# The final norm of a decoder layer, moved into the last expert group of its mixture-of-experts stage

## The reference

```python
def moe_ffn(h, w_router, b_router, w_gu, b_gu, w_down, b_down):
    ...
    xs = hf[tok]
    gu = lax.ragged_dot(xs, w_gu, group_sizes) + b_gu[sorted_e]
    gate, up = jnp.split(gu, 2, axis=-1)
    ...
    act = (up + 1.0) * (gate * jax.nn.sigmoid(SWIGLU_ALPHA * gate))
    out = lax.ragged_dot(act.astype(h.dtype), w_down, group_sizes) + b_down[sorted_e]
    out = out * weights.reshape(-1)[order][:, None]
    y = jnp.zeros((T, D), dtype=out.dtype).at[tok].add(out)

def reference(...):
    ...
    x = x + g2 * moe_ffn(h, ...)
    return rmsnorm(x, norm_f)
```

## Time and profile before

| | |
|---|---|
| median of three runs | 4119.27 us (4119.03 to 4123.2) |
| profiled execution | 4121.83 us, its span 4120.1 us |
| PE busy | 95% of the span |
| DVE, ACT, POOL busy | 57%, 37%, 14% |
| mean granted clock of TensorE | 0.976 |
| moved by DMA | 763.09 MB, mean 185 GB/s |

### The profile page before, as it was taken

How to read it: one execution, slowest core, us unless ns; L and a number is a source line. 1 busy time by engine, 2 the same in 40 slices (tenths; PEclk the granted TensorE clock), 3 DMA queues, 4 the chain that set the end, 5 groups by cost and what they waited for, 6 DMA issues and landing times. The chain is left out here.

```text
span 4120.1 us, 64304 instructions
## 1 busy us (share of the span) xinstructions
PE 3904.0 (95%) x18356; PEld 3205.4 (78%) x18357; DVE 2352.0 (57%) x3725; ACT 1530.1 (37%) x2258; POOL 567.1 (14%) x600
## 2 busy tenths in 40 slices
PE   7999999898979999999999999999999999999993
PEld 4888788787868878878778888878888788888782
DVE  5263342795765764554675666586565656444742
ACT  3222321662223542342453444364343434322532
POOL 1110110111221111101110201111110211111102
PEclk9999999899989999999999999999999999999997
DMA  6442441764345774565684777597575856544826
GB/s 240 156 133 87 156 142 57 251 208 153 133 143 186 244 266 122 153 221 137 201 280 165 222 241 229 151 344 226 167 222 177 258 166 220 163 122 114 268 96 188
DMA packets 347524, 763.09 MB, mean 185 GB/s; under 512 B 29849, under 2 KB 29906, under 8 KB 342818
## 3 DMA queue, kind: packets, MB, share of 16 engines
q1 hardware_dynamic: 289138, 600.04, 42.3%
q0 software_dynamic: 55120, 151.68, 15.0%
q10 hardware_dynamic: 3200, 10.53, 0.6%
HBM read 653.81 MB, written 108.33 MB: 185 GB/s over the span
## 5 line engine op out<-in xcount | busy, mean ns | idle before, releaser
L1860 ACT CAST weights_split<-weights_raw 128x1024 fp32r<-128x1024 f32 x420 | 431.4, 1054 | 536.3 <-PE tok_bank_acc L118 487.2
L116 PE MATMUL tok_bank_acc<-weights_first,weights_split 128*128 128x512 f32 x1264 | 506.2, 401 | 11.4 <-DVE weights_first L1953 9.3
L1953 DVE TENSOR_TENSOR weights_split<-weights_raw,weights_split 128x1024 fp32r<-128x1024 f32 x420 | 490.7, 1220 | 22.0 <-ACT weights_split L1860 13.0
L116 PE MATMUL tok_bank_acc<-weights_split 128*128 128x512 f32 x1264 | 498.4, 394 | 0.8 <-DVE weights_split L1953 0.8
L1953 DVE TENSOR_TENSOR weights_first<-weights_raw,weights_first 128x1024 fp32r<-128x1024 f32 x416 | 483.8, 1219 | 20.7 <-ACT weights_first L1860 18.8
L117 PE MATMUL tok_bank_acc<-weights_split 128*128 128x512 f32 x1264 | 495.6, 392 | 0.0
L118 PE MATMUL tok_bank_acc<-weights_split 128*128 128x512 f32 x1264 | 495.4, 392 | 0.0
L118 PE MATMUL tok_bank_acc<-weights_first,weights_split 128*128 128x512 f32 x1264 | 494.3, 391 | 0.0
L117 PE MATMUL tok_bank_acc<-weights_first,weights_split 128*128 128x512 f32 x1264 | 493.7, 391 | 0.0
L1838 POOL DMA_INDIRECT y_rows<-tok_act_row,tok_token x123 | 199.6, 1622 | 2130.3 <-DVE tok_act_row L2022 2080.7
L1860 ACT CAST weights_first<-weights_raw 128x1024 fp32r<-128x1024 f32 x416 | 425.5, 1050 | 168.8 <-PE tok_bank_acc L118 125.9
(11 more groups left out here) (327 smaller groups left out, 6594.1 us busy)
## 6 DMA issues: line engine op xcount, KB each, us to landing
weights_raw<-in_w_gu SPq DMA_DIRECT2D x560, 512.0 KB
weights_raw<-in_w_down SPq DMA_DIRECT2D x280, 512.0 KB
tok_bias<-in_b_gu SPq DMA_DIRECT2D x35, 1024.0 KB
early_w_raw<-in_w_in POOLq DMA_DIRECT2D x14, 2048.0 KB, 11.1
proj<-pro_stage SPq DMA_DIRECT2D x112, 256.0 KB, 2.0
pro_w_ada<-in_w_ada POOLq DMA_DIRECT2D x64, 256.0 KB, 3.5
mix_late<-proj SPq DMA_DIRECT2D x48, 256.0 KB, 3.7
mod_w_ada<-in_w_ada SPq DMA_DIRECT2D x8, 1024.0 KB, 16.0
```

The costliest lines, as they stand in the source:

```text
L116: nc.tensor.matmul(out, act_hi, w_hi, start=first, stop=False)
L1860: nc.scalar.copy(whi[c % 2][:, j * SK:(j + 1) * SK], raw[:, n % RAW]).then_inc(hi_done, 1)
L1953: nc.vector.tensor_tensor(wlo[c % 2][:, rows], raw[:, n % RAW], whi[c % 2][:, rows], ALU.subtract).then_inc(lo_done, 1)
```

## The change

The finish phase is gone as a phase. What it does is written into the turn of the last group (`G.nT < 1`) of the tokens phase, on the same engines but for the stores, which SP issues.

- **SP**, behind the last piece loads: waits until the group's tokens and shares are taken out of `rec`, loads norm_f into that buffer, waits until all scatters of earlier groups have landed, and loads y tile by tile into the eight weight slots, tile i when piece 16 + i is split. The 16 tiles go in four batches of four (`BATCH`): the stores of batch 0 and 1 must have landed before tiles 8 to 11 and 12 to 15 are loaded into their slots.
- **ACT** squares and takes roots by batch (`tiles_rms`): batch 0 behind the last weight copy, batches 1 to 3 behind the last activation copy. The squares are written to the PSUM bank `tx`; sums and roots lie in parts of `bias`.
- **DVE** inverts and multiplies in place (`tiles_out`): batch 0 in front of `weigh(NGU, 0)`, batches 1 to 3 behind the additions of the first half and in front of `weigh(NGU + 1, 0)`.
- **The tokens of the last group** are not scattered with addition. POOL gathers their sums so far from y into `xs` (eight gathers). DVE adds each weighed half (`add_prior`), ACT squares the whole rows, DVE normalizes them, and POOL writes them to `out` by index, when all stores of tiles have landed, so that they replace what the tiles left there. POOL waits for these writes inside the group's turn.
- The waits for `y_out` at POOL's end are gone, and `weigh(NGU + 1, t)` of the other groups stands inside their `nT > 0` block.

```diff
+                with sp.If(G.nT < 1):
+                    sp.wait_ge(token_set, g + 1)
+                    sp.sem_inc(wait_carrier, 1)
+                    sp.wait_ge(share_set, g + 1)
+                    sp.dma_start(norm_f, A["norm_f"].partition_broadcast(P)).then_inc(nf_in, 16)
+                    for half in range(2):
+                        sp.wait_ge(y_out[half], G.landed(0))
+                        sp.sem_inc(wait_carrier, 1)
+                    def load_tile(i):
+                        for half in range(2):
+                            sp.dma_start(raw[:, i % RAW, half], y_t[half][:, i]).then_inc(fin_in[i // BATCH], 16)
+                    def store_tiles(b):
+                        for i in range(b * BATCH, (b + 1) * BATCH):
+                            sp.wait_ge(z_done, i + 1)
+                            sp.dma_start(out_t[:, i], whole(i)).then_inc(fin_out[b], 16)
+                    for i in range(RAW):
+                        sp.wait_ge(lo_done, G.pieces(PIECES * NCH - RAW + i + 1))
+                        load_tile(i)
+                    for b in range(2):
+                        store_tiles(b)
+                        sp.wait_ge(fin_out[b], 16 * BATCH)
+                        for i in range(RAW + b * BATCH, RAW + (b + 1) * BATCH):
+                            load_tile(i)
+                    for b in range(2, NT // BATCH):
+                        store_tiles(b)
...
+                with pool.If(G.nT < 1):
+                    pool.wait_ge(tx_done, G.before + G.T + 1)
+                    for t in range(GT):
+                        with pool.If(G.T > t):
+                            for half in range(2):
+                                pool.indirect_dma_start(
+                                    out=xs[:, t, half * N:(half + 1) * N], out_offset=None, in_=keep["y"][half],
+                                    in_offset=bass.IndirectOffsetOnAxis(ap=token[:, t:t + 1], axis=0)
+                                    ).then_inc(prior_in, 16)
+                    for done in fin_out:
+                        pool.wait_ge(done, 16 * BATCH)
+                    for t in range(GT):
+                        with pool.If(G.T > t):
+                            pool.wait_ge(last_row, t + 1)
+                            pool.indirect_dma_start(
+                                out=out_rows, out_offset=bass.IndirectOffsetOnAxis(ap=token[:, t:t + 1], axis=0),
+                                in_=xs[:, t], in_offset=None, bounds_check=S - 1, oob_is_err=False).then_inc(row_out, 16)
+                    pool.wait_ge(row_out, G.T * 16)
-        for half in range(2):
-            pool.wait_ge(y_out[half], total * 16 + 16)
...
+                def square_sum(rows, i):
+                    nc.scalar.activation(junk, rows, ACT.Square, accum_out=ssq[:, i:i + 1]).then_inc(sq_done, 1)
+                    act.wait_ge(sq_done, i + 1)
+                def tiles_rms(b):
+                    act.wait_ge(fin_in[b], 32 * BATCH)
+                    for i in range(b * BATCH, (b + 1) * BATCH):
+                        square_sum(whole(i), i)
+                    cols = slice(b * BATCH, (b + 1) * BATCH)
+                    nc.scalar.activation(rms[:, cols], ssq[:, cols], ACT.Sqrt, scale=1.0 / D,
+                                         bias=const("eps")).then_inc(rms_done, 1)
...
                 for n in range(5 * PIECES + PIECES // 2, 6 * PIECES):
                     weights_hi(g, n, G.chunks_before(NGU))
+                with act.If(nT < 1):
+                    tiles_rms(0)
                 for t in range(1, GT):
                     with act.If(G.T > t):
                         activations_hi(1, t)
...
+                with act.If(nT < 1):
+                    for b in range(1, NT // BATCH):
+                        tiles_rms(b)
+                    for t in range(GT):
+                        with act.If(G.T > t):
+                            act.wait_ge(sum_done, G.T + (t + 1))
+                            square_sum(xs[:, t], NT + t)
+                            nc.scalar.activation(rms[:, NT + t:NT + t + 1], ssq[:, NT + t:NT + t + 1], ACT.Sqrt,
+                                                 scale=1.0 / D, bias=const("eps")).then_inc(last_rms, 1)
...
                 for n in range(5 * PIECES + PIECES // 2, 6 * PIECES):
                     weights_lo(g, n)
+                with dve.If(nT < 1):
+                    tiles_out(0)
                 weigh(NGU, 0)
...
+                with dve.If(nT < 1):
+                    dve.wait_ge(prior_in, G.T * 32)
+                    for t in range(GT):
+                        with dve.If(G.T > t):
+                            add_prior(NGU, t)
+                    for b in range(1, NT // BATCH):
+                        tiles_out(b)
+                    for t in range(GT):
+                        with dve.If(G.T > t):
+                            weigh(NGU + 1, t, last=True)
+                            add_prior(NGU + 1, t)
+                    for t in range(GT):
+                        with dve.If(G.T > t):
+                            i = NT + t
+                            dve.wait_ge(last_rms, t + 1)
+                            nc.vector.reciprocal(rms[:, i:i + 1], rms[:, i:i + 1]).then_inc(last_inv, 1)
+                            dve.wait_ge(last_inv, t + 1)
+                            nc.vector.scalar_tensor_tensor(out=xs[:, t], in0=xs[:, t], scalar=rms[:, i:i + 1], in1=norm_f,
+                                                           op0=ALU.mult, op1=ALU.mult).then_inc(last_row, 1)
...
-def phase_finish(nc, k, A, keep):
...
-        run(phase_finish)
```

More of the change, by code:

```diff
@@ L1696, in expert_programs, with whole @@
     rows_left, LEFT = keep["rows_left"], 5
+    (nf_in, sq_done, rms_done, inv_done, z_done, prior_in, sum_done, last_rms, last_inv, last_row,
+     row_out) = k.sems("nf_in sq_done rms_done inv_done z_done prior_in sum_done last_rms last_inv last_row row_out")
+    BATCH = 4
+    fin_in = [k.sem(f"fin_in{b}") for b in range(NT // BATCH)]
+    fin_out = [k.sem(f"fin_out{b}") for b in range(NT // BATCH)]
+    y_t = [a.rearrange("(t p) n -> p t n", p=P) for a in keep["y"]]
+    out_t = keep["out"].rearrange("o (t p) d -> p (o t) d", p=P)
+    out_rows = keep["out"].rearrange("o s d -> (o s) d")
+    norm_f = rec[:].bitcast(F32).rearrange("p q c -> p (q c)")
+    junk = tx[:].rearrange("p a b c -> p (a b c)")
+    def whole(n):
+        return raw[:, n % RAW].rearrange("p s n -> p (s n)")
     y_out = [y_out0, y_out1]
@@ L1816, in gpsimd @@
         pool.wait_ge(rest_in, 16)
-        count, total = field(pool, 0, COUNT, NG), field(pool, 0, TOTAL, NG * GT)
+        count = field(pool, 0, COUNT, NG)
         with pool.Fori(0, NG) as g:
@@ L1832, in gpsimd @@
                 pool.sem_inc(wait_carrier, 1)
-                for c in (NGU, NGU + 1):
+                with pool.If(G.nT > 0):
+                    for c in (NGU, NGU + 1):
+                        for t in range(GT):
+                            with pool.If(G.T > t):
+                                pool.wait_ge(read_done, G.chunk_tile(c, t))
+                                pool.sem_inc(wait_carrier, 1)
+                                pool.indirect_dma_start(
+                                    out=keep["y"][c - NGU],
+                                    out_offset=bass.IndirectOffsetOnAxis(ap=token[:, t:t + 1], axis=0),
+                                    in_=weighted_at(c, t), in_offset=None, compute_op=ALU.add
+                                    ).then_inc(y_out[c - NGU], 16)
@@ L2010, in activations_lo, with tiles_out, add_prior, weigh @@
                     nc.vector.tensor_tensor(alo[:, t, s], ta[:], ahi[:, t, s], ALU.subtract).then_inc(alo_done, 1)
-                def weigh(c, t):
+                def tiles_out(b):
+                    cols = slice(b * BATCH, (b + 1) * BATCH)
+                    dve.wait_ge(rms_done, b + 1)
+                    nc.vector.reciprocal(rms[:, cols], rms[:, cols]).then_inc(inv_done, 1)
+                    dve.wait_ge(inv_done, b + 1)
+                    if b == 0:
+                        dve.wait_ge(nf_in, 16)
+                    for i in range(b * BATCH, (b + 1) * BATCH):
+                        nc.vector.scalar_tensor_tensor(out=whole(i), in0=whole(i), scalar=rms[:, i:i + 1], in1=norm_f,
+                                                       op0=ALU.mult, op1=ALU.mult).then_inc(z_done, 1)
+                def add_prior(c, t):
+                    cols = slice((c - NGU) * N, (c - NGU + 1) * N)
+                    dve.wait_ge(read_done, G.chunk_tile(c, t))
+                    nc.vector.tensor_tensor(xs[:, t, cols], xs[:, t, cols], weighted_at(c, t), ALU.add).then_inc(sum_done, 1)
+                def weigh(c, t, last=False):
                     dve.wait_ge(mm_done, G.chunk_tile(c, t))
@@ L2018, in weigh @@
                         dve.wait_ge(y_out[1], G.landed(0))
-                    if c == NGU + 1 and t == 1:
```

(16 more changed lines are left out.)

54 lines of the change are left out of this document (2 added, 52 removed).

## The result

The changed kernel takes 4462.0 us in the median (4457.3 to 4464.8), the kernel before 4119.6 in the same session: a ratio of 1.0829, with a 95% interval of 1.0816 to 1.0842. It is 8.3% slower, where 0.6% faster was forecast. The profiled execution has a span of 4455.6, which is 335.5 more than the 4120.1 of before.

The account below looks back on a forecast made before the run. With PE 95% busy, only the 65.3 us behind the last weighing, mostly the DMA-bound finish phase, could be won. The new chain gave a span of 4095.7, 24.4 shorter: 4119.3 - 24.4 = 4094.9 us, range 4083 to 4109.

Parts of the forecast that it names:

- only the last 65 us can be won: End of kernel: PE is 95% busy, so only the 65.3 us behind the last weighing can be shortened.
- The last stage: Last group: the chain goes through the batches, not PE, from the first half's last weighing at 4039.0 to the end.
- the loads: Reload of batch 3's slots: eight 256 KB loads after batch 1's stores land, 7.5 us, between 6.3 and 12.5.
- the tail: Behind the row writes: landing 3.7, POOL's 12 empty turns 7.3, drain 1.9, handshakes and clearing 1.5 us.
- The row write: POOL's indirect DMA of a tile's rows in the last group: 1.3 to 1.9 us apart, fourth starting at 4080.3.
- The stall of the first batch: Last group: batch 0 stalls PE 5.1 us, plus 0.8 for a lower clock, moving everything behind by 5.9.
- For 34 earlier groups … I take 1 in all, 0 to 7.: Earlier turns: engines but PE pass one or two more branches per turn, costing 1 us in all, 0 to 7.
- rival 1: Loop bodies outgrow what stays loaded, DVE or ACT refetches each turn: +68 us, 4163; chance 0.06.
- It doesn't do what it says: Last group: one early wait undoes the overlap, tiles start after PE, 4111 to 4120 us; chance 0.04.
- slow clock: PE's clock stays at 1.2 GHz from the last-group stall on, 4127 us; chance 0.02.
- dearer hand-overs: Last group: slower loads, indirect row writes and first entry into skipped code, 4105 us, up to 4111; chance 0.16.
- The signs given for a wrong prediction: Fetches between groups, earlier PE waits grown beyond 1 us, no DVE gap before batch 3, clock below 1 over 4 us.

Follow-up runs that it names:

- behind_no_root: The changed kernel with DVE's second last-group block behind its loop and Identity in place of Sqrt: 4107.6 us, ratio 0.9969 to the kernel before.
- all_behind: The changed kernel with DVE's and ACT's last-group work behind their loops, loops over the group count, second halves between batches: 4091.9 us, ratio 0.9934 to the kernel before.

## Why the prediction was wrong

**What bounds the kernel, and that only the last 65 us can be won.** Nearly right about the gain, and blind to the loss. The last turn and what follows got 14.0 shorter, and would have got 22.6 shorter without the 8.6 of fetches and loads in that turn (below); 25.4 was forecast (24.4, and the 1 that the earlier turns were to cost). A kernel whose PE is 95% busy has little idle time to win in the loop, but all of the loop to lose.

**The last stage.** This was the bulk of the sum, and it holds. From DVE's last weighing of the first half on, timeline of DVE, SP, ACT and POOL in the kernel after:

```profile
4397.07 0.75 DVE L2128 SCALAR_TENSOR_TENSOR tok_act_row<-tok_bank_acc,tok_share,tok_g 128x512 f32<-128x512 f32 x1 [4.18 <-PE tok_bank_acc L118]
4397.74 2.48 DVE L2116 TENSOR_TENSOR tok_rows<-tok_rows,tok_act_row 128x512 f32<-128x512 f32 x4
4400.15 0.17 DVE L2104 RECIPROCAL tok_bias<-tok_bias 128x4 f32<-128x4 f32 x1
4400.35 4.87 DVE L2109 SCALAR_TENSOR_TENSOR weights_raw<-weights_raw,tok_bias,tok_rec 128x1024 f32<-128x1024 f32 x4
...
4408.20 3.66 SPq L1813 DMA_DIRECT2D weights_raw<-y_rows  x8
...
4417.35 1.03 ACT L1958 ACTIVATE tok_bank_tx<-weights_raw 128x1024 f32<-128x1024 f32 x1 [12.64 <-DMA weights_raw<-y_rows]
...
4422.40 0.18 DVE L2104 RECIPROCAL tok_bias<-tok_bias 128x4 f32<-128x4 f32 x1 [12.18 <-ACT tok_bias L1967]
...
4437.33 1.28 DVE L2193 SCALAR_TENSOR_TENSOR tok_rows<-tok_rows,tok_bias,tok_rec 128x1024 f32<-128x1024 f32 x1
...
4439.77 0.97 POOL L1903 DMA_INDIRECT out<-tok_rows,tok_token  x1 [0.30 <-issue]
```

| step | forecast us | measured us |
|---|---|---|
| weighing to the end of four additions | 3.2 | 3.1 |
| products of batch 1 | 5.1 | 5.0 |
| their stores landed, first reload issued | 2.9 | 3.0 |
| eight loads, to the first square of batch 3 | 7.5 | 9.2 |
| squares and root | 5.1 | 5.0 |
| products of batch 3 | 5.2 | 5.0 |
| four pairs of weighing and addition | 5.6 | 5.6 |
| row norms | 5.7 | 5.6 |
| to the fourth row write | 1.0 | 1.2 |
| row write to the end | 14.4 | 15.8 |
| **sum** | **55.7** | **58.5** |

The chain runs through batch 3 as forecast, with the DVE gap (12.18, ended by ACT, and that by a load) where it was said to be. Two terms were small: the loads by 1.7, the tail by 1.4. The row write, of which no row existed, costs 1.0 to 1.4, 1.4 to 1.7 with the gap between two. Its landing of 3.7 to 4.3 is near the forecast 3.7, and the drain behind the empty turns took 2.64 for 1.9, beyond its bound of 2.3; these two are nearly all of the tail's 1.4.

**The stall of the first batch.** PE in the kernel after; then stretches of two us with the columns of the earlier trace rows, the granted clock third from the right:

```profile
4379.96 0.79 PE L116 MATMUL tok_bank_acc<-weights_first,tok_a_hi 128*128 128x512 f32 x1 [4.82 <-DVE tok_a_lo L2098]
```

```profile
4380.00:4382.00 2.00, 2.00 (x5) 1.61 (x6) 0.00 (x0) 0.00 (x0) 0.00 (x0) 0.50 1.03 420
4382.00:4384.00 2.00, 2.00 (x7) 1.52 (x6) 0.00 (x0) 0.00 (x0) 0.00 (x0) 0.50 0.64 260
4384.00:4386.00 2.00, 2.00 (x11) 1.64 (x10) 0.75 (x1) 0.32 (x1) 0.00 (x0) 0.80 0.23 27
4386.00:4388.00 2.00, 2.00 (x11) 1.65 (x10) 0.69 (x1) 1.55 (x2) 0.00 (x0) 1.00 0.99 352
```

The stall is 4.8 for 5.1 forecast. The clock behind it is at its lower level, 1.2 GHz, for the four us to 4384. The forecast had read only two us behind the 2.07 us stall that it took for a measure, and the next two are low as well, with the granted clock at 0.61:

```profile
3996.00:3998.00 2.00, 2.00 (x7) 1.54 (x7) 0.00 (x0) 0.00 (x0) 0.00 (x0) 0.61 0.00 0
```

From the stalled matmul (4379.96) to the last weighing of the half it is 17.1 us against 14.8 before, so 2.3 for the clock and not 0.8. For the size of both together behind_no_root is the clean case, since its ACT has no table loads in the turns and its DVE no fetches. From DVE's turn start to that weighing it takes 125.2 against 119.3, so 5.9 more, the forecast to the tenth, but by two errors that cancel: its PE gets to the stalled matmul 3.0 later than before, not 5.1, for a stall of 4.5, since it is ready for it 1.5 earlier in the turn than the kernel before, and takes 2.9 more behind it, not 0.8. In the changed kernel the way is 14.5 longer. The other 8.6 are put down to the fetches and loads, which the last turn has like every other.

**"For 34 earlier groups … I take 1 in all, 0 to 7."** This is the step that failed: 349.5. Of the 359.9 us between the forecast span and the measured one, 348.5 are this term, 8.6 the same causes in the last turn, and 2.8 the last stage's own. It was costed by the branches that an engine passes, and what it left out has two parts.

*The instruction fetches* were rival 1, and the mechanism was described right: the jump back refetches, and PE pays where splitting is DVE-bound. The count was low, 230 instructions and 100 more where the listing has 281 and 356, but that did not decide: 330 is beyond the cliff as well. What failed is the chance of 0.06. Its argument, that PE's longer body turns without fetches (it does, 837 instructions), says nothing of DVE, and the Trainium skill, cited beside it, let a body of 330 fit. The Trainium skill, page Runtime: NRT & Kernel Launch, section Instruction fetch mechanics, gives an engine other than PE room for 512 instructions, filled in blocks of 256. Here a body of 308 listed instructions does not stay, and the measurement decides. The block size leaves a way in which both hold: a body longer than one block can lie in three of them, where two fit. That is a reading of the Trainium skill, and no run tests it. The other half of that section, that a taken branch to a target outside what is loaded stalls for a fetch, agrees with what the trace shows at every jump back. The price was low too: 3.0 for a fetch where the gap is 3.3 at its shortest and 4.6 in the mean, and two thirds of the turns on the path, where PE waits for split weights 33 times in 34 turns (23 and 10 times up to 4263). So 68 was priced for 163.

*The table loads* were no rival at all. The prediction costed the load once, at 1.28 in the last group, as if a table were loaded when the root is reached. The row was read for its duration and not for the question of who places it. The kernel before had kept the root out of the loop, in a phase of its own, and the earlier trace rows shows its one load there; that no load stood in 34 turns of activations was a sight worth as much as the absence of fetches in the earlier trace rows, and it would have raised the question.

**"It doesn't do what it says", slow clock, dearer hand-overs.** The first two did not come about: the overlap works, and the clock is back at its upper level, 2.4 GHz, in the stretch from 4386. Of the third some 3 us did (the loads and the tail). The signs given for a wrong prediction did name what happened: instruction fetches between groups, and PE's waits in earlier groups grown beyond 1 us. A third sign came too, a clock below 1 for more than 4 us behind the stall, but it is worth only the 2.3 above. Table loads were not among the signs.

**What the change was worth.** Without its two side costs, 12.9 us (behind_no_root); with the empty turns and the order in the last group mended as well, 28.6 (all_behind). The 12.7 between behind_no_root and the forecast is for the most part that DVE has to run through its 12 empty turns before it reaches the work behind the loop, which the forecast had beside other work; DVE in that kernel:

```profile
4047.72 2.50 DVE L2116 TENSOR_TENSOR tok_rows<-tok_rows,tok_act_row 128x512 f32<-128x512 f32 x4 [10.24 <-issue]
```

In all_behind the same gap is 1.07. How its further gain divides between that, the order and ACT's place was not tried apart.

## What to carry to other kernels

Code for one special turn is paid in every turn of a run-time loop even if it is never run there: look at the listing's length of each engine's loop body (DVE's cliff lay between 293 and 308 listed instructions here, in a loop at this place), and at whether the block brings ScalarE a function of another table set than the loop's. Put such code behind the loop, where the program is straight; the same work cost 342 us inside and, in a better order, gave 29 outside. When the profile of before shows none of some event (fetch, table load) in a loop, ask what keeps it away, since that is what a change can break.

## What the runs showed of the hardware beyond that

- The fetch is all or nothing: 29 fetches at 293 instructions, 201 at 308, 323 and 358, each of 8 KB, five for a turn, for 127 to 151 us in 35 turns.
- A never-run root makes 400 table loads of 1283 ns in 35 turns. ACT is less than half busy with them, and the kernel still loses 183 us, since 158 of them stand in front of the activations that DVE and then PE wait for.
- The two costs hit different waits of PE and add up: 127 and 183 alone, 323 together.
- PE's stall of 4.8 us in the last group was followed by at least four us at 1.2 GHz, and over the whole changed kernel the lower mean clock adds 109 us to PE's busy time at an equal count of matmuls, nearly a third of the loss.
